# Recurrence: vectors brought to token order by products with the identity on 64 by 64 tiles instead of transposes over the whole array

## What is computed

```python
def rwkv7_step(S, inp):
    r_t, dec_t, k_t, v_t, kk_t, a_t = inp
    sa = jnp.einsum('bhij,bhj->bhi', S, -kk_t)
    S = (S * dec_t[:, :, None, :]
         + sa[..., None] * (kk_t * a_t)[:, :, None, :]
         + v_t[..., None] * k_t[:, :, None, :])
    y = jnp.einsum('bhij,bhj->bhi', S, r_t)
    return S, y
...
_, y = lax.scan(rwkv7_step, S0, seq)
```

## Time and profile before

| what | value |
|---|---|
| time, median of 3 runs | 2526.11 us (2523.8 to 2527.6) |
| the profiled execution | 2526.39 us, its span 2524.7 us |
| mean granted TensorE clock | 0.979 |
| TensorE busy, share of the span | 95% |
| recurrence stage, from pair 0's first transpose to the end of the last pair | 984.9 to 1152.9 us |
| transposes at L2111 | 128 records, 17.23 us busy |

### The profile page before, as it was taken

The page is one execution under the profiler, slowest core; times in us unless marked ns, Lnnn a source line. Parts: engine busy times, 40 slices in busy tenths (PEclk is TensorE's granted clock), DMA queues, the critical chain, the costliest instruction groups (busy, mean ns, idle before and its releaser), DMA issues.

```text
span 2524.7 us, 34816 instructions
## 1 busy us (share of the span) xinstructions
PE 2405.5 (95%) x13680; PEld 1892.8 (75%) x13680; DVE 1129.9 (45%) x1852; ACT 926.2 (37%) x1542; POOL 1005.3 (40%) x584
## 2 busy tenths in 40 slices
PE   7999999999989888888999999999999999999998
PEld 5775667888866667775887888888667787888887
DVE  5113754203134567525433563362589333552462
ACT  3554653213236444324433322123333534322222
POOL 4341445444442222113553545345324444444344
PEclk9999899999999999989999999999999999999999
DMA  3212002223321110003321223222213221223222
GB/s 125 67 64 92 17 18 92 95 97 100 131 75 42 50 59 22 3 3 128 126 84 59 90 94 117 84 94 89 84 50 109 84 84 59 97 92 112 84 100 67
DMA packets 55588, 198.08 MB, mean 78 GB/s; under 512 B 6551, under 2 KB 8727, under 8 KB 54683
## 3 DMA queue, kind: packets, MB, share of 16 engines
q1 hardware_dynamic: 54509, 192.65, 22.5%
q10 hardware_dynamic: 941, 3.53, 0.4%
HBM read 194.06 MB, written 2.10 MB: 78 GB/s over the span
## 4 chain that ended last, share of the span: by engine, by line
PE 47%; DVE 6%; ACT 1%; issue 0%; DVEq 0%; ACTq 0%
PE ps L370 11%; PE ps L371 11%; PE ps L372 11%; DVE ps L2875 4%; PE ps L445 3%; PE ps L446 3%; PE ps L447 3%; PE ps L2718 1%; PE ps L2741 1%; PE ps L2888 1%; DVE ps L3037 0%; PE ps L2487 0%; PE ps L2728 0%; PE ps L2932 0%; PE ps L2518 0%; PE ps L2491 0%
## 5 line engine op out<-in xcount | busy, mean ns | idle before, releaser
L469 POOL TENSOR_TENSOR w_lo<-raw,w_hi 128x1024 fp32r<-128x1024 f32 x342 | 819.1, 2405 | 1008.1 <-ACT w_hi L461 1008.0
L370 PE MATMUL ps<-ahead_hi,w_hi 128*128 128x512 f32 x1216 | 481.6, 396 | 2.0 <-issue 2.0
L372 PE MATMUL ps<-ahead_hi,w_lo 128*128 128x512 f32 x1216 | 474.0, 390 | 0.0
L371 PE MATMUL ps<-ahead_lo,w_hi 128*128 128x512 f32 x1216 | 473.8, 390 | 0.0
L461 ACT ACTIVATE w_hi<-raw 128x1024 fp32r<-128x1024 f32 x342 | 352.9, 1049 | 169.4 <-PE ps L447 91.0
L370 PEld LDWEIGHTS ps<-ahead_hi,w_hi 128*128 128x128 f32 x1216 | 228.7, 188 | 53.3 <-issue 6.4
L371 PEld LDWEIGHTS ps<-ahead_lo,w_hi 128*128 128x128 f32 x1216 | 228.7, 188 | 50.7 <-issue 4.1
L372 PEld LDWEIGHTS ps<-ahead_hi,w_lo 128*128 128x128 f32 x1216 | 228.6, 188 | 48.0
L736 DVE TENSOR_TENSOR x_stream<-x_stream,ps 128x512 f32<-128x512 f32 x79 | 54.3, 687 | 468.0 <-PE ps L372 278.0
L3009 ACT ACTIVATE ffn_s<-ps 128x512 f32<-128x512 f32 x44 | 26.4, 599 | 322.2 <-DVE ps L3037 322.2
L445 PE MATMUL ps<-ffn_a_hi,w_hi 128*128 128x512 f32 x342 | 133.5, 390 | 3.0 <-DVE ffn_a_lo L3042 2.9
(11 more groups left out here) (415 smaller groups left out, 4395.1 us busy)
## 6 DMA issues: line engine op xcount, KB each, us to landing
raw<-in_wall SPq DMA_DIRECT2D x346, 512.0 KB, 3.3
x_stream<-in_x SPq DMA_DIRECT2D x8, 256.0 KB, 8.0
cw<-in_cmp_w SPq DMA_DIRECT2D x1, 2048.0 KB, 8.6
out_y<-x_stream SPq DMA_DIRECT2D x16, 128.0 KB, 1.9
lora_a<-in_lora_a ACTq DMA_DIRECT2D x1, 1152.0 KB
dist<-in_consts SPq DMA_DIRECT2D x1, 1088.0 KB, 11.7
lora_b<-in_lora_b ACTq DMA_DIRECT2D x1, 1024.0 KB
mem<-in_mem SPq DMA_DIRECT2D x1, 1024.0 KB, 4.9
```

Of the source, the lines that this page charges most:

```text
L370: pe.matmul(out, hi, src.hi[:, t, 0:width], start=first, stop=False)
L371: pe.matmul(out, hi, src.lo[:, t, 0:width], start=False, stop=False)
L372: return pe.matmul(out, lo, src.hi[:, t, 0:width], start=False, stop=last)
L469: e.tensor_tensor(self.w.lo[:, s, :], self.raw[:, s, :], as_float(self.w.hi[:, s, :]), ALU.subtract).then_inc(lo_r.sem, 1)
```

## The change

The single transpose of 128x128 becomes four matmuls on 64x64 tiles: the 64x64 piece of the vector is the weight, the matching 64x64 piece of the identity moves, and the piece lands in its quadrant of the output. The four quadrants are taken in the order that the other 64x64 products have. Since two row halves of the array may not write one bank, head hh goes to a bank of its own: vectors 0 and 1 share banks 3 and 4 (256 columns of each), vectors 2 and 3 share banks 5 and 6. So ScalarE reads each vector from two banks, and its copies wait for both vectors of a pair of banks: `by_token` of n = 1 for n = 0 too, and of n = 3 for n = 2. All four destinations in SBUF stay as they were.

```diff
@@ -2108,7 +2108,10 @@
         for n in range(first, last):
             src = (self.RA[:, 1, p, :], self.rate[:, p, :], self.K[:, p, :], self.vv[:, p, :])[n]
             for i in range(NB):
-                mm = pe.transpose(k.ps[:, 3 + n, self.chunk(i)], src[:, self.chunk(i)], k.ident)
+                for e, hh in ((0, 0), (1, 1), (1, 0), (0, 1)):
+                    o, at, c = self.half(hh), P * i + 64 * e, 256 * (n % 2) + 64 * i
+                    mm = pe.matmul(k.ps[self.half(e), 3 + 2 * (n // 2) + hh, c:c + 64], src[o, at:at + 64], k.ident[o, o],
+                                   start=True, stop=True)
             done(mm, "by_token")
 
     def tokens_scalar(self, act, p):
@@ -2118,15 +2121,15 @@
             wait(act, "small", KD)
             act.wait_ge(self.v_used.sem, self.v_used(KD))
         for n in range(4):
-            wait(act, "by_token", 4 * p + n + 1)
-            sums = k.ps[:, 3 + n, :]
+            wait(act, "by_token", 4 * p + 2 * (n // 2) + 2)
+            b, c = 3 + 2 * (n // 2), 256 * (n % 2)
+            sums = k.ps[:, b:b + 2, c:c + 256].rearrange("p h (i c) -> p h i c", i=NB)
             if n == 0:
-                out, sums = self.AX[:, :, :, 0:64], sums.rearrange("p (i h c) -> p h i c", i=NB, h=2)
+                out = self.AX[:, :, :, 0:64]
             elif n == 1:
                 out = self.PM[:, :, 0:64].rearrange("p (h i) c -> p h i c", h=2)
-                sums = sums.rearrange("p (i h c) -> p h i c", i=NB, h=2)
             else:
-                out, sums = (self.KT, self.VT)[n - 2][:, :, :], sums.rearrange("p (i t) -> p i t", i=NB)
+                out = (self.KT, self.VT)[n - 2][:, :, :].rearrange("p i (h c) -> p h i c", h=2)
             done(act.activation(out, sums, ACT.Copy), "by_token_taken")
```

## The result

The changed kernel takes **2534.35 us** (median of 9 executions, 2530.68 to 2538.37), the kernel before, run beside it, 2527.54 us (9 executions, 2522.44 to 2529.24). The ratio is 1.0030, with a 95% interval of 1.0019 to 1.0041: **slower by 0.3%**, where 2524.2 was forecast and 2530.0 was the end of the range. In the changed kernel the lines of the stage stand 3 further down: tokens at L2113, products at L2151, state steps at L2256, masks at L2160.

What follows compares the result with a forecast made beforehand. Bound by a TensorE-VectorE chain, with 2.31 us a pair before the products becoming 2.03. Seven pairs gain 0.28 us each, pair 0 loses 0.06: 1.9 us, so 2526.11 goes to 2524.2 us, range 2520.5 to 2530.0.

Steps and rivals of the forecast that it cites:

- What bounds the kernel: Chain between TensorE and VectorE; TensorE's work from `Q` to the first products lies on the path, 2.31 us a pair.
- Removed: TensorE, before the products: 16 transposes a pair go, 1.76 us; 0.17 us idle before state steps belongs to tile changes.
- state steps: Steps 1 and 2 on TensorE, now among tiles of their own shape: 0.10 us taken for step 1, upper bound 0.27.
- copies: ScalarE's copies wait for a second vector, but cover stays (0.8 us for `PM`); reading two banks should cost nothing.
- Rival B: State steps on TensorE: the 0.17 us gaps stay, 1.2 us slower, 2527.4 us; chance 0.09.
- Added: Token products on TensorE: 128 records a pair at 15.1 ns, 1.93 us, against 1.75 us for the transposes.
- rival C: Token records on TensorE go at 27.5 ns, not 15.1: 10.8 us slower, 2536.9 us; chance 0.12 with milder forms.
- Pair 0: First pair of the stage: 128 records take 1.93 us against 1.87 for its transposes, 0.06 us lost.
- The clock: Granted clock in the pairs: where its fall meets a pair is luck, 2 us allowed in the range.
- Rival D: Stage's granted clock stops falling because token work keeps it up: 12.0 us more gained, 2512.2 us; chance 0.05.
- The rule against the change: Skill asks for transposes, which skip arithmetic; if products cost that array time, only four quadrants at once pay for it.

Runs made afterwards that it cites:

- with a steady clock: Fillers (products nobody reads, in TensorE's gaps) added to the kernel before, 2513.47 us, and to the changed kernel, 2519.76 us; these hold the clock up.
- the transposes twice: The kernel before with every transpose issued twice, same result: 2545.55 us, ratio to before 1.0065 to 1.0101.
- the repeats: The changed kernel and the kernel before measured again, with nothing different in the built programs: 2535.09 us and 2527.13 us.
- the products twice: The changed kernel with every token product issued twice into the same place: 2565.78 us, ratio to before 1.0143 to 1.0177.

## Why the prediction was wrong

**What bounds the kernel**: right. TensorE's work between `Q` and the first products is on the path; what it saved there (0.28 us forecast, 2.31 to 2.03 us measured) arrived at the mask (0.33 us earlier) and at the end of the pair (18.86 to about 18.55 us with a steady clock).

**Removed, state steps, copies**: right. The 0.17 us of idle time went with the tile change; ScalarE's copies cost nothing (`AX` still 0.60 us from two banks) and were never waited for. This agrees with the Trainium skill (TensorEngine Tiling (Array Packing), Key Properties), which says that changing the tiling mode drains TensorE; here the idle time at such a change is 0.17 us on a weight load. Rival B falls.

**Added**: this is the step that failed. It took 15.1 ns a record "with the same shape and the longest run", 60 records, and multiplied it by 128. The pace itself was right, and each group of 32 that no wait falls into has it (0.47 us). What failed is to carry a pace read from 60 records over to a row of 128 with more products behind it, and to take the supply of instructions as free. The row is now 128 token records, some state records and 64 product records without a stop, and TensorE's instructions come at only 27 to 31 ns a record once what is in store has been used. The prediction had the doubt in words, under rival C ("by instructions that don't come fast enough for 128 records in a row", "no model in this trace"), and priced it as a pace for all 128, 10.8 us, with the chance 0.12. What the runs show is in between: most of the row still goes at 15 ns, and where the border of a block falls decides what the rest costs, nothing to 1.4 us of waiting a pair in this kernel. The term "added instructions" was missing from the sum: 224 a pair, 1792 in the stage, 7 packets more. By the runs with a steady clock it costs an estimated 5.8 us against a gain of 2.2. (The sum also has 1.75 us for the transposes where its own rows gave 1.76, which changes nothing.)

**Pair 0**: forecast to lose 0.06 us, it lost the most. Its tokens and products stand in a row with no state steps between them, and the wait was 1.43 us (1.68 with fillers, where the pair took 2.1 us more).

**The clock**: the profiled stage is 7.7 us longer, and with a steady clock 3.6 us; so in these two executions 4.1 us are the clock's. (They differ by 12.0 us in all; the other 4.4 us lie ahead of the stage, which starts at 989.27 instead of 984.91 us, where the kernels are the same.) But the medians show 6.8 us with a falling clock and 6.3 with a steady one, which leaves it half a microsecond. Whether the waits bring further falls is open: the stage of the repeats has a mean clock of 0.92 before and 0.86 after, but two executions of each are too few. Pair 0 is the place to look: it takes 15.77 us at a clock of 1.00 in before and in its repeat, and 18.99 us at 0.91 and 19.87 us at 0.83 in after and its repeat; but with the transposes twice it is at 0.91 as well, without a wait.

**Rival D** was right in its price and wrong as a consequence of the change: with the clock held up the kernel before takes 2513.47 us, where the 12.0 us worked out from the pairs in the earlier trace rows give 2526.1 - 12.0 = 2514.1 (the 2512.2 of the prediction has the 1.9 us of the change in it too). It wants work in the gaps in which the states are waited for. The Trainium skill (TensorE: Matmul & The Clock Gate, Part 4: PE-mode transpose) says that transposes don't count as busy as matmuls do; replacing them all left the mean clock of the stage at 0.87 against 0.89, and the clock still falls in the gaps behind the masks, so here this rule gives nothing.

**The rule against the change** (the Trainium skill, Perfetto Trace Analysis, Transposes: a transpose should be a transpose and not a standard matmul) came out right for the whole change, for another reason than the arithmetic which it names; for half of it the runs show no loss. The array didn't mind; the instructions did, 16 products of four instructions for four transposes of two.

## What to carry to other kernels

Cutting a matmul into quadrants multiplies the instructions, and each has to be fetched: count the records of PE and PEld in a stretch beside their pace, and look for idle times with "issue" inside a group and for packets of the instruction queue before trusting a pace that only a short run shows. If a small part of such a change holds the gain (here the last two vectors, 0.23 of 0.32 us a pair, too little to show in the total time), take that part alone. And where the granted clock falls in a gap that can't be closed, wide products that nobody reads are worth more than the fine work beside it, if they take few instructions.

## What the hardware showed that was not expected

- TensorE's instructions arrive in packets of 16.4 KB, 256 instructions each. Under a dense row (the products twice) the next 256 come after 3.4 to 3.9 us. In after the packet starts 2.3 to 2.9 us before TensorE goes on.
- A short burst is free of this: 32 records in 0.47 us, and up to 187 records in after (pair 7) and 250 with the products twice (pair 4) before TensorE stands still. In other pairs it stands still after 122, by where the block ends.
- A shift of half a block in the instruction stream, by empty instructions ahead of the stage, moves waits of a microsecond from some pairs to others.
- Empty instructions on TensorE cost time of their own: 56 leave it idle for 2.7 to 3.6 us (48 to 64 ns each, three to four of these records), and 128 in a row added 4.7 us of idle time (37 ns each). They can't be used as filling.
- Fillers of 992 columns a pair in four gaps (64 instructions) keep the clock up through nearly the whole stage, 0.99 instead of 0.89, and give 12.6 us.
